# A gated recurrence beside projections: weight splits in halves, squares in later chunks, the key block copied between the exponentials

## The reference

```python
def step(S, inp):
    qc, kc, gc, vc = inp
    cum = jnp.cumsum(gc, axis=1)
    rel = cum[:, :, None] - cum[:, None, :]
    decay = jnp.exp(jnp.where(tri, rel, -jnp.inf))
    A = jnp.einsum('bthk,btshk,bshk->bhts', qc, decay, kc)
    o = (jnp.einsum('bhts,bshv->bthv', A, vc)
         + jnp.einsum('bthk,bhkv->bthv', qc * jnp.exp(cum), S))
    last = cum[:, -1]
    S_new = (jnp.exp(last)[..., None] * S
             + jnp.einsum('bshk,bshv->bhkv', kc * jnp.exp(last[:, None] - cum), vc))
    return S_new, o
```

## Time and profile before

| | us |
|---|---|
| runs of the kernel, median (lowest to highest of 3) | 2424.07 (2423.71 to 2430.54) |
| the profiled execution | 2431.48 |
| its span | 2429.7 |
| DVE busy, share of the span | 1611.9 (66%) |
| ACT busy | 996.2 (41%) |
| POOL busy | 798.7 (33%) |
| mean granted clock of TensorE | 0.989 |

### The profile page before, as it was taken

How to read it: one execution, slowest core, us unless ns; L and a number is a source line. 1 busy time by engine, 2 the same in 40 slices (tenths; PEclk the granted TensorE clock), 3 DMA queues, 4 the chain that set the end, 5 groups by cost and what they waited for, 6 DMA issues and landing times. The chain is left out here.

```text
span 2429.7 us, 46021 instructions
## 1 busy us (share of the span) xinstructions
PE 2320.2 (95%) x18425; PEld 2168.3 (89%) x18425; DVE 1611.9 (66%) x2711; ACT 996.2 (41%) x2072; POOL 798.7 (33%) x1019
## 2 busy tenths in 40 slices
PE   7899999899999999899999899999999999999999
PEld 6788888888888888888888799998999999999999
DVE  5568676767767686776778515417876677667667
ACT  6455555656555555655432402114322222222221
POOL 1034251524334251524344214442322232232222
PEclk9999999999999999999999999999999999999999
DMA  6213022221213021221598523111111111111112
GB/s 268 88 37 106 27 72 79 62 80 48 87 52 98 29 91 58 62 89 45 203 340 318 225 87 114 44 56 39 44 44 52 44 44 44 52 44 48 46 47 94
DMA packets 75343, 213.18 MB, mean 88 GB/s; under 512 B 15738, under 2 KB 24186, under 8 KB 75130
## 3 DMA queue, kind: packets, MB, share of 16 engines
q1 hardware_dynamic: 73978, 206.05, 25.1%
q10 hardware_dynamic: 1152, 4.19, 0.4%
HBM read 175.49 MB, written 26.26 MB: 83 GB/s over the span
## 5 line engine op out<-in xcount | busy, mean ns | idle before, releaser
L170 PE MATMUL h_G<-xn_hi,h_w_hi 128*128 128x344 f32 x1392 | 467.8, 336 | 8.4 <-ACT h_d_oraw L858 5.0
L170 PE MATMUL h_G<-xn_hi,h_w_lo 128*128 128x344 f32 x1392 | 445.2, 320 | 0.0
L170 PE MATMUL h_G<-xn_lo,h_w_hi 128*128 128x344 f32 x1392 | 444.9, 320 | 0.0
L2299 POOL TENSOR_TENSOR h_w_lo<-h_w_raw,h_w_hi 128x1024 fp32r<-128x1024 f32 x88 | 212.9, 2420 | 397.4 <-ACT h_w_hi L2070 388.1
L2240 PE MATMUL t_ps<-hn_hi,h_w_hi 128*128 128x344 f32 x1032 | 331.1, 321 | 0.0
L2240 PE MATMUL t_ps<-hn_lo,h_w_hi 128*128 128x344 f32 x1032 | 330.3, 320 | 0.0
L2240 PE MATMUL t_ps<-hn_hi,h_w_lo 128*128 128x344 f32 x1032 | 330.2, 320 | 0.0
L1120 POOL TENSOR_TENSOR h_w_lo<-h_w_raw,h_w_hi 128x1024 fp32r<-128x1024 f32 x58 | 146.3, 2523 | 493.8 <-ACT h_w_hi L738 448.3
L170 PEld LDWEIGHTS h_G<-xn_hi,h_w_hi 128*128 128x128 f32 x1392 | 263.8, 190 | 45.8 <-issue 17.1
L170 PEld LDWEIGHTS h_G<-xn_lo,h_w_hi 128*128 128x128 f32 x1392 | 262.3, 188 | 4.8 <-issue 0.7
L170 PEld LDWEIGHTS h_G<-xn_hi,h_w_lo 128*128 128x128 f32 x1392 | 262.2, 188 | 0.0
(11 more groups left out here) (367 smaller groups left out, 5540.1 us busy)
## 6 DMA issues: line engine op xcount, KB each, us to landing
h_w_raw<-in_w_in SPq DMA_DIRECT2D x72, 512.0 KB, 4.4
h_w_raw<-in_w_ffn SPq DMA_DIRECT2D x66, 512.0 KB, 3.6
h_d_ada_w<-in_w_ada SPq DMA_DIRECT2D x32, 512.0 KB, 5.0
g_kp<-in_cache_k SPq DMA_DIRECT2D x32, 512.0 KB, 7.0
g_vp<-in_cache_v SPq DMA_DIRECT2D x32, 512.0 KB, 5.4
h_w_raw<-in_w_mix SPq DMA_DIRECT2D x24, 512.0 KB, 3.7
x<-in_xT SPq DMA_DIRECT2D x16, 516.0 KB, 7.3
n_ada_w<-in_w_ada SPq DMA_DIRECT2D x16, 512.0 KB, 12.3
```

Source lines behind the costliest of these rows:

```text
L170: ins = eng.matmul(out, w[:, k * P:(k + 1) * P], x[:, k, columns], start=(k == 0 and n == 0), stop=(k == n_k - 1 and n == 2))
L2299: pool.tensor_tensor(wlo[buf(n)][:, :], raw[n % 2][:, :], whi[buf(n)][:, :].bitcast(F32), ALU.subtract).then_inc(w_lo.sem, 1)
```

## The change

In ScalarE's list `levels` is cut in three: the five fine levels, the top level, the two edge exponentials (the last one signals `lv_exp`). The copy of the key block now stands between the top level and the edges (in chunk 0 ahead of the top level too). The last sigmoid moves from ahead of the chunks to behind the exponentials of chunk 0, and its use on VectorE behind the operands of chunk 1.

In GpSimd's list the five small copies move from ahead of the chunks into chunk 0; the squares move to chunks 2 and 5; each weight split of the recurrence becomes two instructions over 512 columns, in chunks 0 and 1, 3 and 4, 6 and 7, each behind the differences and ahead of the cosine product. Only the second half signals `lo_done`. TensorE's and SyncE's lists stay.

```diff
+HALF_AT = {0: (13, 0), 1: (13, 1), 3: (16, 0), 4: (16, 1), 6: (19, 0), 7: (19, 1)}
+SQUARES_AT = (2, 5)
...
-            def levels(h, k):
+            def fine_levels(h, k):
 
                 act.wait_ge(lv_diff.sem, lv_diff.at(h, k + 1))
                 act.wait_ge(lv_k.sem, lv_k.at(h, k))
+                act.activation(L[:, 1:FINE + 1, :], df[:, :, :], ACT.Exp, scale=-1.0)
+
+            def top_level(h, k):
+
                 at = k * P
-                act.activation(L[:, 1:FINE + 1, :], df[:, :, :], ACT.Exp, scale=-1.0)
                 act.activation(L[:, LEVELS - 1, 0:HALF], braw[:, at:at + HALF], ACT.Exp, scale=-1.0, bias=braw[:, at + HALF - 1:at + HALF])
                 act.activation(L[:, LEVELS - 1, HALF:P], braw[:, at + HALF:at + P], ACT.Exp, bias=neg_mid[:, k:k + 1])
+
+            def edge_levels(h, k):
+
+                at = k * P
                 act.activation(L[:, 0, :], braw[:, at:at + P], ACT.Exp, scale=-1.0, bias=braw[:, at + P - 1:at + P])
                 act.activation(L[:, LEVELS, :], braw[:, at:at + P], ACT.Exp).then_inc(lv_exp.sem, 1)
...
-                sigmoid(h, len(SIGMOID) - 1)
 
                 for k in range(NB):
                     if k + 1 < NB:
-                        levels(h, k + 1)
+                        fine_levels(h, k + 1)
+                        if k:
+                            top_level(h, k + 1)
                     act.wait_ge(rec_done.sem, rec_done.at(h, k + 1))
                     act.activation(kht[:, :], kht_ps, ACT.Copy).then_inc(kht_ready.sem, 1)
+                    if k + 1 < NB:
+                        if k == 0:
+                            top_level(h, 1)
+                        edge_levels(h, k + 1)
+                    if k == 0:
+                        sigmoid(h, len(SIGMOID) - 1)
...
+            def split_half(h, n, half):
+
+                t, at = SPLIT_AT[n], slice(half * KT * P // 2, (half + 1) * KT * P // 2)
+                w, r = slot(t % NTL), 0 if t == NTL else t % 2
+                if half == 0:
+                    raw_loaded(pool, h, t)
+                    pool.wait_ge(hi_done.sem, hi_done.at(h, t))
+                    used_wait(pool, h, t)
+                ch.sync()
+                ins = pool.tensor_tensor(wlo[w][:, at], raw[r][:, at], whi[w][:, at].bitcast(F32), ALU.subtract)
+                if half == 0:
+                    ch(ins)
+                else:
+                    ins.then_inc(lo_done.sem, 1)
...
                 for k in range(NB):
                     if k + 2 < NB:
                         differences(h, k + 2)
+                    if k in HALF_AT:
+                        split_half(h, *HALF_AT[k])
+                    if k == 0:
+                        pool.wait_ge(sig_used.sem, sig_used.at(h, 9))
+                        pool.wait_ge(piece_read.sem, piece_read.at(h, 9))
+                        for n, src in (("f", fc), ("kk", kk), ("qh", qh), ("ib", ib), ("og", og)):
+                            ch(kept(n, src, h))
+                        ch.sync()
+                        pool.sem_inc(sample_rec.sem, 1)
+                    if k in SQUARES_AT:
+                        pool.wait_ge(pv_read.sem, pv_read.at(h, NB))
+                        pool.wait_ge(o_normed.sem, o_normed.at(h, 0))
+                        squares(h, oraw, SQUARES_AT.index(k))
                     if k < 6 and not no_next(h):
                         pool.wait_ge(piece_read.sem, piece_read.at(h, 12 + k + 1))
                         pool.wait_ge(qk_turned[k].sem, qk_turned[k].at(h, 4))
                         pool.tensor_tensor(rg[k % 2][:, :], rg[k % 2][:, :], cos[:, cols(k % NP)], ALU.mult).then_inc(qk_cos.sem, 1)
-                    for n in REC_PIECES[k]:
-                        split_next(h, n)
```

## The result

The changed kernel took 2457.59 us (median of 4 runs, 2450.11 to 2460.79) against 2424.23 (4 runs, 2423.71 to 2430.54) of the kernel before on the same chip: a ratio of 1.0125, 95% interval 1.0113 to 1.0137. That is slower by 33 us, where 29 were predicted.

The account below looks back on a forecast made before the run. TensorE bounds the kernel, with VectorE setting a chunk's pace. Seven heads +23.8, clock +7.2 and last head -2.0 make +29.0 us: 2460.5 from the profiled 2431.48, 2453 on the median, range 2430 to 2472.

Parts of the forecast that it names:

- The deciding step: Chunk 4: tile 6's split ends later, holding tile 7's load and piece 16's transfers; VectorE's rotary product 4.25 us later.
- collision: Chunk 5: GpSimd's squares and cosine product meet VectorE's L1338 and L1323; 0.75 us a head taken, 0 to 1.7 possible.
- Chunks 0 to 3: Earlier key copy and the first split's halves gain 1.6 us a head by chunk 4's start; bounds 1.0 and 2.5.
- Clock: TensorE falls to half clock behind the new stalls in all seven heads; sum +7.2 us, bounds 0 and 17.
- Last head: It turns no pieces, so it only gains: its 2.5 us of waits fall by about 2.
- Squares in chunk 2: Chunks 2 and 3: cosine products move 1.0 to 1.4 us, costing nothing; 0.5 us a head if not.
- This chain had no slack: Chunk 4 before: piece 16's transfers came last; GpSimd waited 2.24 us for them, VectorE 0.83 for GpSimd.
- What would show it: Profile signs: tile 7's load 2.5 us later, GpSimd waiting about 5, TensorE 3 to 4.5 for AT in chunk 5.
- The turned piece isn't late: Rival: piece 16's transfers are not held or land in time, chunks 4 and 5 keep TensorE's pace; about 2396 us; chance 0.14.
- More half clock: Rival: two half-clock stretches a head cost 17 us in place of 7.2, with 1.7 of collision; 2469 us; chance 0.12.
- Only part shows: Rival: the lateness is at its lower bound and the clock drops no more often; +4, about 2428 us; chance 0.07.
- no effect of halving: Rival: chunks 0 and 1 are held by something else, so halving gains nothing; about 2464 us; chance 0.05.

Follow-up runs that it names:

- turn_first: Changed kernel with the four transfers of piece 16 ahead of the load of tile 7 in SyncE's list: 2408.59 us, 0.9918 of the kernel before.
- second_half_early: Changed kernel with the second half of tile 6's split ahead of chunk 4's differences instead of behind them: 2418.12 us, 0.995 of the kernel before.
- whole_tile6: Changed kernel with tile 6's split whole again in chunk 3, behind the cosine product: 2414.23 us, 0.9934 of the kernel before.
- halves_only: Kernel before with only the six half splits of the change, nothing else of it: 2461.74 us, 1.0129 of the kernel before.
- whole_in_chunk4: Kernel before with tile 6's split undivided but moved to chunk 4, between differences and cosine product: 2475.87 us, 1.0187 of the kernel before.
- turn_first_tile5_behind: Changed kernel with piece 16's transfers ahead of tile 7's load, tile 5's halves and five copies behind the cosine products: 2398.0 us, 0.9867 of before.
- before_turn_first: Kernel before with piece 16's transfers moved ahead of the load of tile 7 in SyncE's list: 2431.17 us, 1.0007 of the kernel before.
- no_halves: Changed kernel with whole splits behind the cosine products in chunks 0, 3 and 6, as before: 2433.82 us, 1.0021 of the kernel before.
- load_behind_turn: Changed kernel, SyncE still waiting for tile 6's split but then issuing piece 16's transfers ahead of the load: 2453.33 us, 1.0098 of the kernel before.
- keep_busy: Changed kernel with 20 unused matmuls added in chunk 5 of heads 0 to 6, ahead of TensorE's AT wait: 2453.63 us, 1.0098 of before.

## Why the prediction was right

The sign, the size and the mechanism were right. By its own steps, head 3 where nothing else is said:

- **The deciding step.** Second half ended 6.52 us into chunk 4 (628.61 - 622.09), predicted 6.3. From there to the cosine product 6.26, predicted 5.43. To the rotary product 0.94 for 0.96. Together 13.72 for 12.7. turn_first, second_half_early and whole_tile6 take the step away and the loss goes; halves_only has nothing but the halves and has all of the loss; whole_in_chunk4 has it without any halves.
- **From the rotary product to chunk 6**: 5.68, predicted 5.74 and 0.75 of collision. The collision did not happen. When GpSimd's squares (L1191) began, the first of VectorE's two instructions had passed and the second had begun 0.15 us before; neither was stretched:

```profile
638.56 0.29 DVE L1372 TENSOR_TENSOR h_AT<-h_spot_near_sum,h_spot_same_mask 128x128 f32<-128x128 f32 x1
639.10 0.28 DVE L1357 TENSOR_TENSOR h_b_LQ<-h_fc,h_qh 128x128 f32<-128x128 f32 x1
...
639.25 1.04 POOL L1191 TENSOR_TENSOR h_d_rstd_o<-h_d_oraw 128x512 f32<-128x512 f32 x1 [0.24 <-POOL h_b_level_diff L1185]
```

  Two wrong terms, +0.8 of landing and -0.75 of collision, cancel here: from chunk 4 to chunk 6 it was 19.40 for 14.18, +5.2, predicted +5.0; the mean of the seven heads, chunks 4 and 5 of the table, is +4.7. With the start of chunk 4 at -1.62 that is +3.05 a head without the clock, predicted 3.4.
- **Chunks 0 to 3**: -1.6 by the start of chunk 4 predicted, -1.62 measured (chunk 2 without its clock). The wait ahead of chunk 1 went, L1338 (now L1372) of chunk 0 took 0.29 for 1.01. Yet the working was wrong in one place: halving was to end the trouble of the rotary product in chunk 0. GpSimd in chunk 0 of head 3 after, and VectorE behind it:

```profile
600.04 1.55 POOL L1163 TENSOR_TENSOR h_w_lo<-h_w_raw,h_w_hi 128x512 fp32r<-128x512 f32 x1 [0.34 <-PE h_G L170]
...
602.47 0.93 POOL L1234 TENSOR_TENSOR h_d_rg<-h_d_rg,h_cos 128x344 f32<-128x344 f32 x1 [0.24 <-POOL keep_s_og L1170]
...
603.43 0.59 DVE L1254 TENSOR_TENSOR h_d_rt<-h_d_rt,h_sin 128x344 f32<-128x344 f32 x1 [2.98 <-POOL h_d_rg L1234]
```

  The stretch of 2.16 us (2.68 less 0.52) beside a wait of 1.16 became a wait of 2.98 beside a stretch of 0.07: 3.32 against 3.05. The prediction took the stretch off and did not follow the wait. Nor did the second half meet L1323 (now L1357) in chunk 1 for 0.7: it never takes over 0.35 us in this kernel. So chunk 1 kept both its stalls, 1.02 and 1.31, and the 1.6 came from chunk 0 alone. turn_first_tile5_behind is the correction, and the 1.0 us a head that it finds in chunk 1.
- **Clock**, mis-sized. Predicted +7.2 as 10.1 + 2.9 - 5.8. In chunk 6 it cost 7 x 1.84 = 12.9; in chunk 2 the stalls were not cut, so it stayed, and grew to 7.4 (what the seven chunks 2 take above 6.4 each); 12.9 + 7.4 - 5.8 = +14.5. The fall behind the stall came in every head, as said, and nearer to the upper bound of 17.
- **Last head**: -1.7, predicted -2.0. **Squares in chunk 2**: nothing there was predicted, and chunks 2 and 3 move by no more than the clock.
- **"This chain had no slack"** held in the direction in which it was used: from the rotary product to chunk 6 it took 5.68 us after and 5.74 before, so what made that product later moved chunk 6 by as much. It does not hold the other way. In before_turn_first VectorE's wait of 0.83 is gone, chunk 6 comes 0.26 us sooner, and nothing is gained by chunk 7.
- **What would show it.** The load was 4.5 us later in its chunk (6.59 for 2.13), where the list said 2.5; that figure was at odds with the prediction's own 4.25, which is what counts. GpSimd waited 5.8 a head (5 said), VectorE 5.4 to 7.1 (5 said), TensorE 3.3 to 4.9 (3 to 4.5 said) and another 0.6 to 1.3 ahead of chunk 6 (2 in the working), L1103 in total 35.9 (30 said). The rotary product never went over 1.8 us, in all of the program; after, in the first fence, and before, in the second (x42, then ns of one: shortest, median, longest):

```profile
L1254 DVE TENSOR_TENSOR h_d_rt<-h_d_rt,h_sin x42: 516/518/591, 179.1 to 1064.0; 128x344 f32<-128x344 f32 x42
```

```profile
L1220 DVE TENSOR_TENSOR h_d_rt<-h_d_rt,h_sin x42: 516/518/2689, 177.8 to 1029.2; 128x344 f32<-128x344 f32 x42
```

  The Trainium skill (SBUF — State Buffer, "Who interferes with whom") says that a VectorE instruction with two SBUF inputs contends with a GpSimd instruction that reads SBUF, and calls this contention an exclusive lock. These runs agree: with no split beside it, the longest of 42 is 0.59 us; beside one, 2.69 in no_halves. The ends tell more than the lengths: the product ended 0.37 us behind the end of the whole split in no_halves (589.80 and 589.43), and 0.37 and 0.38 behind the end of a half in turn_first_tile5_behind (GpSimd's halves there ended at 574.34 and 580.87).
- **The rivals.** *The turned piece isn't late* is excluded by the trace and, as a mechanism, is just what turn_first makes true: the prediction priced it at 2396, 28 below, and turn_first came 20 below. Without the clock, chunk 6 there comes 2.5 us a head sooner, where that rival had 2.9; the clock gives back 2.7 us in all and not 6, since chunk 2 still falls in two heads; and chunk 6 itself takes 8.06 us for 7.69, with a wait of 0.64 ahead of chunk 7 in five heads, which the rival did not have. *More half clock* was half right: one such chunk in each head, but a dear one, and chunk 2 besides. *Only part shows* and *no effect of halving* did not come about.

## What to carry to other kernels

Before an instruction is made to end later, ask which other queues wait for its semaphore, and what stands *behind* the waiting instruction in each: here a load that nobody needed before chunk 6 held four transfers that GpSimd, VectorE and TensorE needed at once, and moving one line in SyncE's list turned 1.3% slower into 0.8% faster. A long GpSimd product cut in halves takes its stretching off VectorE, but a half (or five small copies) put ahead of what VectorE waits for turns the stretch into a wait of about the same length: count both. And a sum that agrees may do so by errors that cancel; check each term against its own row.

## What the runs showed of the hardware that was not expected

- **Transfers behind a load.** From the end of the split to usable data it took 5.43 us before and 6.26 after in head 3, with the load ahead of the transfers in both; 1.3 us of the 6.26 is the load going first (load_behind_turn). After, the transfers of piece 17 follow at once (eight issues in 5.46 us, for 7.97 before, where they came later); whether that makes the 0.8 us more was not tried.
- **The clock after one stall.** Waits of 3.3 to 4.9 us and 0.6 to 1.3 with a short chunk's end between brought the granted clock down in the chunk behind them in seven heads of seven, at 1.4 to 2.5 us each; and 3.4 us of matmuls put into the first wait, with 0.5 to 1.95 and 1.3 to 2.1 us of waiting left, prevented that in one head of seven. In chunk 2, behind two waits of 1.0 and 1.3, it fell in some heads and not in others (6.39 and 9.16 us for one chunk): in four of seven in the change, two in turn_first, five in load_behind_turn, none in keep_busy, with the same two waits in all of them. Why those, stays open; it means that several microseconds between two profiled executions can be this and not the edit.
